# One stage of an attention kernel: compressed values in 64 columns, their products in tiles of 32 rows by 64 outputs, and a new order of TensorE's work around them

## The reference, cut to what matters

```python
def compress_blocks(a, pe, w1, w2):            # a: keys or values, 2 groups of width 64
    blocks = ...                               # 15 overlapping blocks of 32 tokens, plus pe
    return jax.nn.gelu(flat @ w1) @ w2         # -> 15 compressed rows of width 64 per group

# per query block of 128 tokens, 2 groups x 4 heads
s   = q . k_cmp - slope * dist                 # scores against 15 compressed keys
p_c = masked_softmax(s)
o_c = p_c @ v_cmp                              # 15 compressed values
o_s, o_w = ...                                 # selected blocks and window: here all 256 tokens
o   = gate0 * o_c + gate1 * o_s + gate2 * o_w
x   = x + concat([o, mem_attend(mq, mem_k, mem_v)]) @ w_out
```

## Time and profile before

| | us |
|---|---|
| median of 3 runs | 895.11 (895.02 to 895.35) |
| the profiled execution | 895.46 |
| its span, first to last instruction | 893.8 |
| PE busy | 888.1 (99% of the span) |
| DVE busy | 647.5 (72%) |
| ACT busy | 495.3 (55%) |

### The profile page before, as it was taken

How to read it: one execution, slowest core, us unless ns; L and a number is a source line. 1 busy time by engine, 2 the same in 40 slices (tenths; PEclk the granted TensorE clock), 3 DMA queues, 4 the chain that set the end, 5 groups by cost and what they waited for, 6 DMA issues and landing times.

```text
span 893.8 us, 18696 instructions
## 1 busy us (share of the span) xinstructions
PE 888.1 (99%) x7883; PEld 862.6 (97%) x7883; DVE 647.5 (72%) x1189; ACT 495.3 (55%) x851; POOL 42.0 (5%) x50
## 2 busy tenths in 40 slices
PE   8999999999999999999999999999999999999998
PEld 7999999999999998899999999999988999999998
DVE  6987657877767789785887767678688586565664
ACT  6764555564645557575665555547457464444451
POOL 1000001000000000000100000000142000000000
PEclk9999999999999999999999999999999999999999
DMA  8753343555365444632546554553162265546541
GB/s 317 283 178 119 139 147 141 220 225 216 146 233 192 160 171 160 232 140 95 201 184 253 194 203 183 201 213 128 73 226 101 99 224 204 195 180 216 199 153 48
DMA packets 26002, 160.68 MB, mean 180 GB/s; under 512 B 3008, under 2 KB 4928, under 8 KB 7360
## 3 DMA queue, kind: packets, MB, share of 16 engines
q1 hardware_dynamic: 25344, 158.45, 48.5%
q10 hardware_dynamic: 576, 1.05, 0.4%
HBM read 158.18 MB, written 1.05 MB: 178 GB/s over the span
## 4 chain that ended last, share of the span: by engine, by line
PE 97%; DVE 1%; DMA 1%; SPq 0%; issue 0%; ACT 0%
PE ps L417 95%; PE ps L433 2%; DMA raw<-in_w 1%; DVE arena L1729 0%; DVE wl L1279 0%; DVE arena L1713 0%; SPq L2586 0%; DVE arena L1785 0%; DVE arena L1804 0%; DVE xt L1475 0%; DVE arena L1726 0%; DVE wl L1495 0%; ACT wh L2221 0%; DVE arena L1708 0%; DVE arena L1722 0%
## 5 line engine op out<-in xcount | busy, mean ns | idle before, releaser
L1279 DVE TENSOR_TENSOR wl<-raw,wh 128x1024 fp32r<-128x1024 f32 x280 | 329.4, 1223 | 124.5 <-ACT wh L2073 124.1
L417 PE MATMUL ps<-xh,wh 128*128 128x256 f32 (+1 forms) x1264 | 352.4, 279 | 0.5 <-DVE wl L1495 0.5
L417 PE MATMUL ps<-xl,wh 128*128 128x256 f32 (+1 forms) x1264 | 350.0, 277 | 0.0
L417 PE MATMUL ps<-xh,wl 128*128 128x256 f32 (+1 forms) x1264 | 350.0, 277 | 0.0
L2073 ACT CAST wh<-raw 128x1024 fp32r<-128x1024 f32 x280 | 277.3, 1047 | 114.7 <-PE ps L417 104.9
L417 PEld LDWEIGHTS ps<-xh,wh 128*128 128x128 f32 x1264 | 237.4, 188 | 2.3 <-DVE wl L1495 0.9
L417 PEld LDWEIGHTS ps<-xl,wh 128*128 128x128 f32 x1264 | 237.4, 188 | 0.1
L417 PEld LDWEIGHTS ps<-xh,wl 128*128 128x128 f32 x1264 | 237.5, 188 | 0.0
L417 PE MATMUL ps<-fh,wh 128*128 128x256 f32 x528 | 145.7, 276 | 0.0
L417 PE MATMUL ps<-fl,wh 128*128 128x256 f32 x528 | 145.7, 276 | 0.0
L417 PE MATMUL ps<-fh,wl 128*128 128x256 f32 x528 | 145.7, 276 | 0.0
(11 more groups left out here) (257 smaller groups left out, 1052.0 us busy)
## 6 DMA issues: line engine op xcount, KB each, us to landing
raw<-in_w SPq DMA_DIRECT2D x144, 1024.0 KB, 4.9
raw<-in_w ACTq DMA_DIRECT2D x4, 256.0 KB, 5.5
xt<-in_x SPq DMA_DIRECT2D x4, 256.0 KB, 6.7
raw<-in_w SPq DMA_DIRECT2D x4, 256.0 KB, 8.1
arena<-in_mem SPq DMA_DIRECT2D x1, 1024.0 KB, 8.3
out<-xt SPq DMA_DIRECT2D x8, 128.0 KB, 1.9
arena<-in_sel SPq DMA_DIRECT2D x3, 256.0 KB, 5.9
small<-in_small SPq DMA_DIRECT2D x1, 623.0 KB, 6.5
```

The source lines that it names most:

```text
L417: return pe.matmul(out, lhsT, rhs, start=start, stop=stop, skip_group_check=True)
L1279: v.tensor_tensor(L[:, s], src[:, s], f32(H[:, s]), ALU.subtract).then_inc(*w_lo.up(split(i, a)))
```

## The change

Values in `vcm` are 64 wide instead of 256. `blocks_out` makes eight products of 32 rows by 64 outputs and 256 columns instead of four of 128 rows by 128 outputs; the rows n*32 go to bank `no0` for n = 0, 1 and to `no1` for n = 2, 3, and to the lower or upper 64 partitions by n % 2. For that the heads of the compressed scores are placed in the order 0, 2, 1, 3, and the gates and the slopes follow. `squeeze(1, 1)` follows `squeeze(1, 0)` at once. `nsa_turn(2)` stands between chunks 5 and 6 of `Bm0`; `kvm` comes after these chunks, with the values' products ahead of the keys'; and `nsa_out(2)` comes ahead of `blocks_scores`. ACT runs `nsa_turned(2)` and then both heads of `nsa_exps(3)`.

```diff
-    gT, kcm, vcm, gt, gh = area(120), area(16), area(256), area(48), area(512)
+    gT, kcm, vcm, gt, gh = area(120), area(16), area(256)[:, 0:64], area(48), area(512)
...
+        PLACE = (0, 2, 1, 3)
...
-                    last = mm(ps[f"cs{g}"][:, n * 64 + j * 16:n * 64 + j * 16 + 15],
+                    at = n * 64 + PLACE[j] * 16
+                    last = mm(ps[f"cs{g}"][:, at:at + 15],
                               bq[r:r + 64, j, (1 - n) * 128:(2 - n) * 128], kcm[r:r + 64, 0:15], True, True)
...
         def blocks_out():
             t.wait_ge(*ps.done("kvm"))
             t.wait_ge(*ps.done("ct"))
-            for j in range(4):
-                name = f"no{j // 2}"
-                last = mm(ps[name][:, j % 2 * 256:j % 2 * 256 + 256], vcm[:, j % 2 * 128:(j % 2 + 1) * 128],
-                          PC2[:, j // 2 * 256:(j // 2 + 1) * 256], False, True)
-                if j % 2:
-                    last.then_inc(*ps.full(name))
+            for odd in range(2):
+                for n in range(4):
+                    name, r, g = f"no{n // 2}", n * 32, n % 2
+                    last = mm(ps[name][g * 64:(g + 1) * 64, odd * 256:(odd + 1) * 256], vcm[r:r + 32, :],
+                              PC2[r:r + 32, odd * 256:(odd + 1) * 256], False, True)
+                    if odd and g:
+                        last.then_inc(*ps.full(name))
...
         squeeze(1, 0, 2)
+        squeeze(1, 1)
         nsa_scores(2)
-        squeeze(1, 1)
         part_f("Bm0", 1, range(0, 4), x_b)
         nsa_scores(3)
         P = ps.open("gT", 0)
...
-        part_f("Bm0", 1, range(4, 8), x_b)
+        part_f("Bm0", 1, range(4, 6), x_b)
+        nsa_turn(2)
+        part_f("Bm0", 1, range(6, 8), x_b)
         P = ps.open("kvm", 2)
         t.wait_ge(*ps.vacant("kvm"))
         t.wait_ge(*ps.done("gT"))
+        for n in range(4):
+            for c in range(2):
+                mm(P[n * 32:n * 32 + 15, 64:128], g4[:, 1, c, n % 2, :], sm("wcv2")[:, c * 64:(c + 1) * 64], c == 0, c == 1)
         for g in range(2):
             for c in range(2):
-                mm(P[g * 64:(g + 1) * 64, 0:15], sm("wck2")[:, c * 64:(c + 1) * 64], g4[:, 0, c, g, :], c == 0, c == 1)
-
-        for n in range(4):
-            for c in range(2):
-                last = mm(P[n * 32:n * 32 + 15, 64:128], g4[:, 1, c, n % 2, :], sm("wcv2")[:, c * 64:(c + 1) * 64], c == 0, c == 1)
+                last = mm(P[g * 64:(g + 1) * 64, 0:15], sm("wck2")[:, c * 64:(c + 1) * 64], g4[:, 0, c, g, :], c == 0, c == 1)
         last.then_inc(*ps.full("kvm"))
-        nsa_turn(2)
+        nsa_out(2)
         blocks_scores(0, (7, 0))
         blocks_scores(1, None)
-        nsa_out(2)
         mem_scores(1, 0, 4, mqB, qB)
...
         for n in range(4):
-            r, a = n * 32, n // 2 * 128 + n % 2 * 64
-            last = v.tensor_copy(vcm[r:r + 15, a:a + 64], ps["kvm"][r:r + 15, 64:128])
+            r = n * 32
+            last = v.tensor_copy(vcm[r:r + 15, :], ps["kvm"][r:r + 15, 64:128])
...
-        nsa_exps(3, (0,))
         nsa_turned(2)
-        nsa_exps(3, (1,))
+        nsa_exps(3)
```

More of the change, by code:

```diff
@@ L1762, in blocks_probs @@
             for n in range(2):
-                w = sc8[:, 32 + n * 8:40 + n * 8].rearrange("p (j g) -> p j g", g=2)
-                gate = gt[:, n * 24:n * 24 + 24].rearrange("p (g j x) -> p j g x", g=2, j=4)[:, :, :, 0]
+                w = sc8[:, 32 + n * 8:40 + n * 8].rearrange("p (odd a g) -> p odd a g", a=2, g=2)
+                gate = gt[:, n * 24:n * 24 + 24].rearrange("p (g a odd x) -> p odd a g x", g=2, a=2, odd=2)[:, :, :, :, 0]
                 last = v.tensor_tensor(w, w, gate, ALU.mult)
@@ L2686, in constants @@
     qs = np.array([[0.125 / slope(j, r // 64) for j in range(4)] for r in range(128)])
-    sl = np.broadcast_to(np.array([slope(j, g) for j in range(4) for g in range(2)]), (128, 8))
+    sl = np.broadcast_to(np.array([slope(j, g) for j in (0, 2, 1, 3) for g in range(2)]), (128, 8))
     ns = np.concatenate([-(128 + t - s), np.where(s <= t, -(t - s), NEG)] + cmp + [qs, sl], 1).astype(f)
```

## The result

| | before | after |
|---|---|---|
| median of 20 runs, us | 895.2 (894.66 to 895.58) | 896.88 (896.42 to 897.46) |
| ratio | | 1.0019 (95% interval 1.0013 to 1.0025) |
| profiled execution, us | 895.46 | 896.86 |
| its span, us | 893.8 | 895.2 |

The change costs 1.68 us. The two groups of 20 do not touch.

A forecast was written before the change was run, and what follows sets the result against it. The prediction took TensorE (PE), busy 99% of the span, as the bound; its delays up to `Bm1` made a shift of 1.85, `blocks_out` gained nothing, so 895.11 + 1.85 = 896.96, called 897.0 us; range 895.6 to 898.6.

The forecast's parts named there:

- Part 1: Second compression in one piece: PE saves 0.14 us, but head 2's scores start 0.86 later and `gT` 0.30 later.
- The relay: Hand-over from PE to DVE to ACT after the second compression, claimed 0.86 us late, making `gT` 0.30 late.
- Part 2: `nsa_turn(2)` inside `Bm0`: PE stands still 0.4 us for bank 5, held until DVE's read of the scores.
- Part 3: After `kvm`: PE idles from about 386.3 to 387.65 us before `nsa_out(2)`; `Bm1` starts at 391.79 instead of 389.96.
- The bank: Bank 2 holds `kvm` until DVE's copies end at 387.49 us, so `nsa_out(2)` waits, with 0.16 for the hand-over.
- Part 4: ACT's new order: `nsa_probs(3)` ends near 391.45 instead of 390.74 us, covered by `Bm1`'s MATMULs; cost nothing.
- Part 5: `blocks_out` four abreast takes 0.9 us less, but PE waits 1.0 for ACT before `mem_out(1, 0)`; gain nothing.
- Rival A: Whole changed stretch: PE's own work decides, 1.1 us less, 894.0; chance 0.12.
- Rival B: At `kvm`: only the wait for bank 2 costs, head 2's scores are not late; shift 1.0, 896.1 us; chance 0.16.
- Rival C: In `blocks_out`: the small tiles run one after another, 3.6 us; shift 3.5, 898.6 us; chance 0.1.
- the bound: For the whole kernel's time: 896.90 us, about 0.2% (1.79 us) up, above which it counts as slower; slower given 0.50.

The follow-up runs named there:

- e2: Kernel before the change with only the second compression in one piece, ahead of `nsa_scores(2)`: 896.86 us against 895.33, ratio 1.0019.
- e11: e2 run again for its spread, on another chip: 896.50 us against 895.28 for the kernel before, ratio 1.0016.
- e3: Changed kernel with `kvm` in bank 7 instead of bank 2: 895.97 us against 895.33 for the kernel before, ratio 1.0006.
- e1: Kernel before with only the new `blocks_out` tiles, `vcm` and order of heads and gates, nothing moved: 895.50 us against 895.33, ratio 1.0002.
- e6: e5 with ACT's copy `mem_turned(1, 0)` ahead of its cast of `Bo1`: 895.88 us against 895.29 for the kernel before, ratio 1.0006.
- e9: e7 with ACT's cast of `Bo1` moved to where ACT waited for `blocks_turn`, and `nsa_high(0)` following `mem_turned(1, 0)`: 894.21 us, ratio 0.9989 to the kernel before.
- e5: Changed kernel with the second compression again in two halves and `kvm` in bank 7: 895.27 us against 895.29 for the kernel before, ratio 1.0000.
- e4: Changed kernel with the second compression again in two halves round `nsa_scores(2)`, `kvm` still in bank 2: 896.27 us against 895.33 for the kernel before, ratio 1.0011.
- e8: e7 with ACT's `nsa_high` ahead of the cast, and DVE's `nsa_low` and `mem_max(1, 2)` ahead of the low part of `Bo1`: 895.57 us, ratio 1.0004 to the kernel before.
- e7: e6 with ACT's `mem_turned(1, 1)` also ahead of `mem_exp(1, 2)`: 895.41 us against 895.29 for the kernel before, ratio 1.0000.

## Why the prediction was right

Forecast 896.96, rounded to 897.0, measured 896.88; a shift of 1.85 against 1.68 (medians) and 1.59 (stage). (The prediction's own places for `Bm1`, 391.79 and 389.96, give 1.83.) Point by point, counted from the squeeze's start:

- *Part 1.* PE saves 0.14: the 32 products and the way to the scores take 1.86 (371.55 to 373.41), as predicted. The relay is 0.86 late: measured 0.86 on DVE and 0.87 on ACT. `gT` 0.30 late: 0.36. e2 and e11 show the edit alone: 0.93 and 0.72, where I had 0.8.
- *Part 2.* 0.4 of standing still within the turn: `nsa_turn(2)` starts at 382.24 and its second half at 383.20, 0.3 more than the 0.65 of the first six; the weight load's wait for DVE's line 1717 is 0.4. `kvm` I had at 13.93, it is at 13.83.
- *Part 3.* The bank: 1.11 of idle, the releaser is DVE's copy, and e3 takes it away by another bank number. This is the largest term, and it was mis-sized by 0.1: I had taken 0.16 for the hand-over with three waits to pass, and it is 0.06. `Bm1` was to start 20.04 after the squeeze and starts at 19.85.
- *Part 4.* Nothing, as forecast: `nsa_turn(3)` has no wait. DVE's `mem_max(1, 0)` is 1.25 late, where I had 1.5.
- *Part 5.* Four abreast, 0.9 less work, and all of it lost at `mem_out(1, 0)`, in the change (1.05 of idle) and alone (e1). Why it was lost was argued then. e6 shows the cause: with the copy ahead of the cast in ACT's run, `mem_out(1, 0)` starts 0.88 earlier. And e9 shows what it takes to keep it: with the cast moved out of the run, 0.90 are there at `mem_out(1, 0)` and 0.71 at the end of the stage (both against e5).

Rival A is refuted by e1 and e2. Rival B, only the bank, is what e4 measures: 0.97, where its sum said 1.0; but the scores were late, so it was not this kernel. Rival C did not happen. The Trainium skill (TensorEngine Tiling (Array Packing), Restrictions and Gotchas) says that different row tiles cannot access the same PSUM bank at once; here the tiles of rows 0 and 32 write bank 3 abreast, and those of rows 64 and 96 bank 2, each pair to different 64 partitions, and there are four steps and not eight. The measurement decides: for outputs on different partitions of a bank the rule did not hold.

What stayed luck: the nearness of 0.08 us, since the sum set out from a median 0.09 lower than that of the 20 runs and its shift was 0.17 too large; and the chance of 0.5 for slower and 0.48 for no change. The shift came out at 0.19% with an interval of 0.13% to 0.25%, on both sides of the bound, and I see nothing in the rows that could have split it better.

## What to carry to other kernels

In a kernel whose bound engine is 99% busy, ask of each edit what work of that engine stands between a hand-over and its return; removing work there may only lengthen the wait, as it did with `blocks_out` (e1), and moving work ahead of a hand-over may make one (e2). A bank's or buffer's order is a dependency like any other: before moving a step up, look at who holds its output's place. And if a gain is lost to an engine that is only half busy, look for where that engine stands idle before its long job, and put the job there; reordering the short jobs round the long one three times gave nothing (e6 to e8), and moving the long one, on top of e7's order, gave 1.1 us over the kernel before (0.7 by the stage).

## What the runs showed of the hardware

- Products of 32 rows by 64 outputs run four abreast: 16 in 1.09 us, the same pace as products of 128 rows by 32 outputs, which also run four abreast (16 in 1.07 before).
- The kernel with only the squeeze in one piece has times in two groups, on both occasions: of 21 executions (e2 and e11), 12 at a mean granted clock of 1.000 took 895.2 to 896.86, and 9 at 0.998 took 897.26 to 898.24. Of 20 executions of the changed kernel, which has the same squeeze and the same late relay, none was under 1.000. An estimate from the mean: 0.002 of 894 us is 1.8 us lost, or 3.6 us at the lower level (1.2 instead of 2.4 GHz), and with the rounding of 0.998 anything from 2.7 to 4.5; the two groups' medians lie 1.4 (e2) and 1.6 (e11) apart. No profiled execution fell into this group, so where the clock fell, and what PE had done before, stays open. In its median e2 is therefore 0.6 above its undisturbed executions (median 896.24), and those are 0.9 over the kernel before, which is what its stage says; those of e11 (median 895.97) are 0.7 over, again as its stage says.
